# A short convolution's first tap on ScalarE in a two-layer block on one core

## Reference

```python
qkv = jax.nn.silu(causal_depthwise_conv(qkv, w_conv_qkv[i]))      # four taps along the tokens, one weight per channel
q, k, v = jnp.split(qkv, 3, axis=-1)                              # 16 heads of 128 each
q, k, v = l2norm(heads(q)), l2norm(heads(k)), heads(v)
beta = jax.nn.sigmoid(b_raw)
o_a = gated_delta_chunked(q, k, v, g_log, beta)                   # uses k and kb = k * beta
```

## Time and profile before

| | |
|---|---|
| median of 3 runs | 2548.47 us (2547.51 to 2551.29) |
| the profiled execution | 2548.92 us, its span 2547.4 us |
| PE busy | 2461.4 us, 97% of the span |
| DVE busy | 1629.1 us, 64% |
| ACT busy | 1155.0 us, 45% |
| POOL busy | 175.4 us, 7% |
| mean granted PE clock | 0.991 of full speed |

### The profile page before, as it was taken

The page is one execution under the profiler, slowest core; times in us unless marked ns, Lnnn a source line. Parts: engine busy times, 40 slices in busy tenths (PEclk is TensorE's granted clock), DMA queues, the critical chain, the costliest instruction groups (busy, mean ns, idle before and its releaser), DMA issues.

```text
span 2547.4 us, 34830 instructions
## 1 busy us (share of the span) xinstructions
PE 2461.4 (97%) x13453; PEld 2046.6 (80%) x13453; DVE 1629.1 (64%) x2146; ACT 1155.0 (45%) x1475; POOL 175.4 (7%) x254
## 2 busy tenths in 40 slices
PE   7999999988999999999999889999999999999997
PEld 6878878867888888788887778888888888888886
DVE  5899999678585766646546655656465544565554
ACT  5444444455353535334445454444444444443443
POOL 3000000153000101001000010000000000000000
PEclk9999999989999999999999999999999999999999
DMA  7566666445343344648655445655565655675563
GB/s 233 187 203 205 211 202 205 156 158 166 117 149 117 133 133 142 212 161 276 235 185 187 165 155 175 207 168 203 171 204 163 224 187 193 205 274 192 188 218 113
DMA packets 226899, 469.75 MB, mean 184 GB/s; under 512 B 12217, under 2 KB 13090, under 8 KB 225634
## 3 DMA queue, kind: packets, MB, share of 16 engines
q1 hardware_dynamic: 214018, 418.57, 49.5%
q0 software_dynamic: 12768, 49.59, 5.6%
HBM read 445.05 MB, written 23.07 MB: 184 GB/s over the span
## 4 chain that ended last, share of the span: by engine, by line
PE 70%; DVE 3%; ACT 2%; issue 1%; POOL 0%; DVEq 0%; ACTq 0%; POOLq 0%
PE acc L2119 60%; PE aux L2265 3%; PE aux L2149 1%; PE aux L2351 1%; PE aux L2355 1%; DVE w_lo L1376 1%; DVE cy L1632 0%; PE aux L2276 0%; ACT w_hi L809 0%; PE aux L2340 0%; PE aux L2350 0%; PE aux L2535 0%; PE aux L2534 0%; PE acc L2442 0%; ACT qT L1053 0%
## 5 line engine op out<-in xcount | busy, mean ns | idle before, releaser
L1376 DVE TENSOR_TENSOR w_lo<-raw,w_hi 128x1024 fp32r<-128x1024 f32 x790 | 973.0, 1235 | 817.1 <-ACT w_hi L809 805.6
L809 ACT CAST w_hi<-raw 128x1024 fp32r<-128x1024 f32 x790 | 827.0, 1051 | 1188.3 <-PE acc L2119 1176.0
L2119 PE MATMUL acc<-w_hi,r1h 128*128 128x512 f32 (+1 forms) x1920 | 764.1, 398 | 7.4 <-DVE r1l L1461 4.4
L2119 PE MATMUL acc<-w_lo,r1h 128*128 128x512 f32 (+1 forms) x1920 | 747.5, 389 | 0.0
L2119 PE MATMUL acc<-w_hi,r1l 128*128 128x512 f32 (+1 forms) x1920 | 747.4, 389 | 0.0
L2119 PE MATMUL acc<-w_hi,r2h 128*128 128x512 f32 x1216 | 477.5, 393 | 2.2 <-DVE w_lo L1376 1.9
L2119 PE MATMUL acc<-w_lo,r2h 128*128 128x512 f32 x1216 | 473.5, 389 | 0.0
L2119 PE MATMUL acc<-w_hi,r2l 128*128 128x512 f32 x1216 | 473.5, 389 | 0.0
L2119 PEld LDWEIGHTS acc<-w_hi,r1h 128*128 128x128 f32 x1920 | 362.6, 189 | 85.8 <-issue 5.1
L2119 PEld LDWEIGHTS acc<-w_hi,r1l 128*128 128x128 f32 x1920 | 362.1, 189 | 76.1
L2119 PEld LDWEIGHTS acc<-w_lo,r1h 128*128 128x128 f32 x1920 | 362.6, 189 | 69.9 <-issue 1.0
(11 more groups left out here) (442 smaller groups left out, 1591.3 us busy)
## 6 DMA issues: line engine op xcount, KB each, us to landing
raw<-in_w_in SPq DMA_DIRECT2D x264, 1024.0 KB, 5.0
raw<-in_w_out SPq DMA_DIRECT2D x32, 1024.0 KB, 4.9
raw<-in_w_br_b SPq DMA_DIRECT2D x16, 1024.0 KB, 4.9
raw<-in_w_br_a SPq DMA_DIRECT2D x16, 1024.0 KB, 5.3
raw<-in_w_ple_gate SPq DMA_DIRECT2D x16, 1024.0 KB, 4.9
raw<-in_w_o_mla SPq DMA_DIRECT2D x16, 1024.0 KB, 4.9
raw<-in_w_o_conv SPq DMA_DIRECT2D x16, 1024.0 KB, 4.9
raw<-in_w_q_b SPq DMA_DIRECT2D x8, 1024.0 KB, 5.1
```

The source lines that it names most:

```text
L809: nc.scalar.copy(w_hi[:, h % HL, 0:n], raw[:, k % RAW, x * HALF:x * HALF + n]).then_inc(hi_ready, 1)
L1376: V.tensor_tensor(w_lo[:, h % HL, 0:n], raw[:, k % RAW, x * HALF:x * HALF + n], w_hi[:, h % HL, 0:n].bitcast(F32), ALU.subtract).then_inc( ...
L2119: ins = T.matmul(acc[:, s, x, 0:n], a[:, kt0 + k, xs_], w[:, h % HL, at], start=start and k == 0 and m == 0, stop=stop and k == kts - 1 an ...
```

## The change

ACT writes the first tap of each convolution (tap 0) into `cy`, right behind the padding copies, in halves 10, 19 and 26. For n = 1 and 2 it first waits for `qk_square`, since DVE still has to sum the squares that lie in `cy`. DVE waits for `tap0_ready` in place of `cpad_ready` and does the 12 steps that are left, spread over the same halves. The small copies of the tap weights (`wq4`, three per group) go from DVE's half 0 to ACT's. DVE signals `ktok_ready` behind the scaled k and `kb_ready` behind k times beta; PE waits for the first ahead of the transposes of `ktok` and for the second ahead of those of `kb`. Four signals that occur once each become one counter, `small_done`; the order in which PE raises it is the order in which they were raised before.

```diff
@@ ScalarE
             def own(ph, hl, i, first):
+                if hl == 0:
+                    for n in range(3):
+                        c.inc(nc.scalar.copy(wq4[:, n], pc[:, bass.ds(i * GH, GH), R_SC + n:N_ROWS:3]))
...
+                for n, (evac, _, pad, (conv, conv_end), silu, back) in enumerate(OWN):
+                    if hl == conv - 1:
+                        if n:
+                            act.wait_ge(sem("qk_square"), i * 2 + n)
+                        c.wait()
+                        for h in range(GH):
+                            ins = A(cy[:, h], cpad[:, h, 0:TOK], ACT.Copy, scale=wq4[:, n, h, 0:1])
+                            if h < GH - 1:
+                                c.inc(ins)
+                        sig(ins, "tap0_ready", i * 3 + (n + 1))
@@ VectorE
             def own(ph, hl, i):
-                if hl == 0:
-                    for n in range(3):
-                        c.link(V.tensor_copy(wq4[:, n], pc[:, bass.ds(i * GH, GH), R_SC + n:N_ROWS:3]))
                 for n, (_, _, _, (conv, conv_end), silu, back) in enumerate(OWN):
                     if hl == conv:
-                        dve.wait_ge(sem("cpad_ready"), i * 3 + (n + 1))
+                        dve.wait_ge(sem("tap0_ready"), i * 3 + (n + 1))
                     if conv <= hl <= conv_end:
-                        steps, m = [(k, h) for k in range(SHORT) for h in range(GH)], conv_end - conv + 1
-                        for k, h in steps[16 * (hl - conv) // m:16 * (hl - conv + 1) // m]:
+                        steps, m = [(k, h) for k in range(1, SHORT) for h in range(GH)], conv_end - conv + 1
+                        for k, h in steps[len(steps) * (hl - conv) // m:len(steps) * (hl - conv + 1) // m]:
                             c.wait(GH - 1)
                             win, w = cpad[:, h, k:k + TOK], wq4[:, n, h, k:k + 1]
-                            if k == 0:
-                                c.inc(V.tensor_scalar(cy[:, h], win, w, None, ALU.mult))
-                            else:
-                                c.inc(V.scalar_tensor_tensor(cy[:, h], win, w, cy[:, h], ALU.mult, ALU.add))
+                            c.inc(V.scalar_tensor_tensor(cy[:, h], win, w, cy[:, h], ALU.mult, ALU.add))
...
                 if hl == 31:
                     dve.wait_ge(sem("cols_ready"), i + 1)
-                    c.link(V.tensor_tensor(th(ktok), th(ktok), over(col(2), DK), ALU.mult))
-                    c.link(V.tensor_tensor(th(kb), th(ktok), over(col(3), DK), ALU.mult))
-                    dve.sem_inc(sem("kb_ready"), 1)
+                    sig(V.tensor_tensor(th(ktok), th(ktok), over(col(2), DK), ALU.mult), "ktok_ready", i + 1)
+                    sig(V.tensor_tensor(th(kb), th(ktok), over(col(3), DK), ALU.mult), "kb_ready", i + 1)
@@ TensorE
             def delta(hl, dv, i=None):
                 if hl == 0:
+                    pe.wait_ge(sem("ktok_ready"), dv(1, 1))
+                    per_head_tr(0, ktok, "kT_tr")
                     pe.wait_ge(sem("kb_ready"), dv(1, 1))
-                    per_head_tr(0, ktok, "kT_tr")
                     pe.wait_ge(sem("vb_ready"), dv(1, 1))
                     per_head_tr(2, kb).then_inc(sem("kbT_tr"), 1)
```

More of the change, by code:

```diff
@@ L103 @@
 TR_GAINS, TR_NARROW, TR_ROWS = range(1, 4)
+SMALL_DECAYS, SMALL_MEAN, SMALL_RSTD, SMALL_P = range(1, 5)
 ROW_SLOT = P // KT
@@ L855, in decays_exp @@
             def decays_exp():
-                act.wait_ge(sem("gc_done"), 1)
+                act.wait_ge(sem("small_done"), SMALL_DECAYS)
                 n16 = TT * HEADS
@@ L977, in own @@
             def own(ph, hl, i, first):
-                for n, (evac, _, pad, (_, conv_end), silu, back) in enumerate(OWN):
+                if hl == 0:
+                    for n in range(3):
+                        c.inc(nc.scalar.copy(wq4[:, n], pc[:, bass.ds(i * GH, GH), R_SC + n:N_ROWS:3]))
+                for n, (evac, _, pad, (conv, conv_end), silu, back) in enumerate(OWN):
                     if hl == back + 1 and n < 2:
@@ L1083, in _ @@
                 if hl == 2:
-                    act.wait_ge(sem("mean_done"), 1)
+                    act.wait_ge(sem("small_done"), SMALL_MEAN)
                     sig(nc.scalar.copy(rows[:], X[:, 0, 0:TOK]), "rows_ready", 1)
                 if hl == 11:
-                    act.wait_ge(sem("rstd_rows"), 1)
+                    act.wait_ge(sem("small_done"), SMALL_RSTD)
                     act.wait_ge(sem("ln_centered"), NJ)
@@ L1151, in evac_square @@
                 act.wait_ge(acc_free[s], freed(ph, bl, i))
-            act.wait_ge(sem("p_tr"), 1)
+            act.wait_ge(sem("small_done"), SMALL_P)
             sig(nc.scalar.copy(pTh[:].rearrange("p a b -> p (a b)"), X[:, 2]), "p_hi", 1)
@@ L2190, in log_decays @@
                         ins = T.matmul(X[:, 3, at:at + HEADS], half_ones[:, n, :], glog[:, x], start=True, stop=True)
-                ins.then_inc(sem("gc_done"), 1)
+                ins.then_inc(sem("small_done"), 1)
             def u_transposed(ph, i):
@@ L2369, in _ @@
                         ins = T.matmul(X[:, 0, 0:TOK], ones_mean[:], y[:, kt], start=kt == 0, stop=kt == KT - 1)
-                    ins.then_inc(sem("mean_done"), 1)
+                    ins.then_inc(sem("small_done"), 1)
                 if 4 <= hl < 4 + NJ:
@@ L2383, in _ @@
                         ins = T.matmul(X[:, 1, x * P:(x + 1) * P], ones_mean[:], rdiag[:, x], start=True, stop=True)
-                    ins.then_inc(sem("rstd_rows"), 1)
+                    ins.then_inc(sem("small_done"), 1)
                 own(ph, hl, 0)
@@ L2423, in _ @@
                     ins = T.transpose(X[:, 2, a * TOK + x * P:a * TOK + (x + 1) * P], ptok[:, x, a * P:(a + 1) * P], ident[:])
-            ins.then_inc(sem("p_tr"), 1)
+            ins.then_inc(sem("small_done"), 1)
             ph = PH["MIX"]
```

## The result

| | before | after |
|---|---|---|
| median, lowest to highest, of 8 runs each, in turn on one chip | 2548.24 us (2547.32 to 2551.29) | 2555.28 us (2552.27 to 2556.96) |
| ratio, 95% interval | | 1.0029 (1.002 to 1.0038) |
| the profiled execution, its span | 2548.92, 2547.4 us | 2552.27, 2550.7 us |
| PE, DVE, ACT busy | 2461.4, 1629.1, 1155.0 us | 2463.7, 1614.3, 1176.3 us |
| mean granted PE clock | 0.991 | 0.990 |

The change makes the kernel slower by 7.0 us, 0.29%. DVE has 14.8 us less to do and ACT 21.3 us more, as intended; PE gains nothing from it.

A forecast was written before the change was run, and what follows sets the result against it. PE, busy for 97% of the span, was taken as the bound, so only its waits could change. +2.8 us (group 0) and +1.9 (groups 1 to 3) gave +4.7: 2553.6 for the execution, 2553.2 for the median, range 2548.5 to 2557.5.

The forecast's parts named there:

- +2.8 for group 0: Group 0: PE starts the decays 3.9 us late, less 0.3 of a wait and 0.8 from q and k.
- +1.9 behind it: Groups 1 to 3: the decays start later by about 0.6 us in each, +1.9 us in all.
- The rounding of half 30: Groups 1 to 3, on ACT: queued behind v's taps, which wait for DVE's sum of squares, it starts 2.27 us late.
- the prediction's own test: Groups 1 to 3: the forecast counts as wrong if the rounding of half 30 starts less than 2 us late.
- The price of the taps: On ACT: four taps of 128x256 with a per-partition scale take 1.65 us, from a range of 1.58 to 2.08.
- Group 0, q: PE's 10.8 us wait for q shrinks by 0.7 us; the next DVE step inherits the first taps' delay from POOL.
- POOL's hold is what matters: Rival, group 0: q's wait shrinks by some 3.5 us instead of 0.7, sum about +1.9, 2550.4 us; chance 0.16.
- Group 0, v: ACT's taps wait for the sum of squares; luh starts 3.9 us late, DVE's lul ends 4.05 late, PE's decays 3.9 late.
- PE's clock adds little: Group 0: a 4 us wait for v would cost about 1 us of clock, mostly while PE would wait for ktok anyway.
- ACT's wait is hidden: Rival, all groups: rounding three halves ahead takes up the 2.27 us, all removals count, −9, 2539.5 us; chance 0.09.
- Little of it shows: Rival: the late rounding is partly taken up, about +1, 2549.5 us; chance 0.10.
- The slower rival: Four taps take 2.08 us, 0.43 more in each of four chains, and group 0's w_lo loses time; +8.5, 2557 us; chance 0.15.

The follow-up runs named there:

- e1_again: The changed kernel measured once more with no edit, for its spread and a second profile: 2556.00 us, ratio 1.0033.
- e2_squares: The changed kernel with ACT's squares of q and k in tile kbe instead of cy, so the taps need not wait: 2547.18 us, ratio 0.9996.
- e3_wait: The kernel before, with only ACT's wait for qk_square added behind the padding copies; no tap moved: 2555.64 us, ratio 1.0029.
- e8_shift: The kernel before, with PE transposing the scaled k twice in each group: 2550.77 us, ratio 1.0015.
- e9_shift3: The kernel before, with PE transposing the scaled k three times in each group: 2553.88 us, ratio 1.0025.
- e5_split: The kernel before with only the split signal (ktok_ready, kb_ready); taps and weight copies stay on DVE: 2546.13 us, ratio 0.9997.
- e6_copies: The kernel of e5_split plus the three small weight copies per group on ACT; all taps on DVE: 2548.43 us, ratio 1.0.
- e7_best: The kernel of e2_squares with v's taps in group 0 alone back on DVE: 2544.59 us, ratio 0.9985.
- e4_v_on_dve: The changed kernel with all four taps of v back on DVE; the rest of the change stays: 2545.66 us, ratio 0.9991.

## Why the prediction came out as it did

**The mechanism was right, and its sum nearly so.** Forecast were +2.8 for group 0 and +1.9 behind it, 4.7 us; the stretches give 3.6 and 1.2, 4.8 us (5.0 in e1_again). That the sums agree to 0.1 us is luck: group 0 cost 0.8 more than forecast and the others 0.7 less. e2_squares and e3_wait show from both sides that ACT's wait for `qk_square` makes it. The chances were a little off: 0.53 went to a change within 0.2%, 0.38 to a slower one, and it is 0.29%.

**Groups 1 to 3, step by step.** Predicted and found: PE's wait for the gated output 1.31 and 1.37 us; for `ktok` 0.43 and 0.42; for the decays' operand 0.54 and 0.32. The wait for the convolved values fell from 0.77 to 0.45. The rounding of half 30 came 1.94 us late against the decays ahead (733.16 - 618.03 against 729.33 - 616.14), not 2.27: the sum of squares itself ended 0.55 us earlier, which fits DVE's fewer steps ahead of it but was not tested. By the prediction's own test (under 2 us is a sign of being wrong) this is just on the wrong side, without consequence: 0.4 us for each group instead of 0.6. PE's waits grew by only 0.5 of these 1.2 us (7.9 to 8.4 over the stretch), and the clock is 1.00 throughout in both kernels; the rest appears as PE's busy time, 407.95 us in place of 406.64 for the same 3463 matmuls. Sets of matmuls behind a wait are recorded a little longer, as the output's transposes (1.09 against 1.03) and the decays (1.10 against 1.02); that this makes the whole rest is not shown.

**The price of the taps** was 1.65 us and is 1.71 to 1.72. The Trainium skill (ScalarE: Activation LUTs, What ACT_TABLE_LOAD costs) gave an estimate of 1.69; the trace agrees to 0.03 us. The nearest row for such a price was in the earlier trace rows and not in the earlier trace rows: eight operations with a scale for each partition, from SBUF to SBUF, at half the columns, 2.45 us.

**Group 0, q.** Forecast -0.7; the wait is 10.2 us where it was 10.8. The rival "POOL's hold is what matters" fell. DVE in the changed kernel:

```profile
525.00 3.57 DVE L1640 SCALAR_TENSOR_TENSOR cy<-cpad,wq,cy 128x256 f32<-128x256 f32 x3
...
532.34 5.78 DVE L1640 SCALAR_TENSOR_TENSOR cy<-cpad,wq,cy 128x256 f32<-128x256 f32 x3
538.04 3.39 DVE L1765 SCALAR_TENSOR_TENSOR lnt<-lnt,lnsq 128x1024 f32<-128x1024 f32 x1
```

Three steps take 3.57 us where four first taps took 3.54, and three take 5.78 where four took 5.94: the delay passed to the next step, and behind the steps to L1765, which takes 3.39 us here and took 1.21 before. The Trainium skill (SBUF — State Buffer, two separate sides) says that a DVE operation with two SBUF inputs waits for the ports shared with POOL while a POOL operation that reads SBUF holds them. The trace agrees: beside POOL's L628 (2.56 us each) two single steps took 2.62 us each, where four take 1.67 us in group 1.

**Group 0, v.** Measured from the `szT` mark, `luh` starts 3.4 us late (130.19 against 126.82), POOL's last column 3.6 late (147.62 against 144.03), the decays 3.6. Forecast were 3.9 less the 0.8 of q and k for the same chain, so 3.1 at that mark. The 0.1 of k was not found, q gave 0.1 less, and the rest of the half microsecond lies between `luh` and POOL's columns. The wait of 0.3 for bf came back, but behind the mark.

**Where PE spent those 3.6 us was wrong in part.** PE's waits in group 0 grew only by 1.3 us (from 17.9 to 19.2, the same view for 478 to 622 us). The others were spent at the lower clock. Behind the starts of k's and v's transposes, before and after:

```profile
585.00:588.00 3.00, 3.00 (x19) 2.59 (x18) 1.42 (x2) 2.97 (x6) 0.00 (x0) 1.00 1.06 321
...
606.80:609.80 3.00, 2.94 (x17) 2.62 (x18) 2.02 (x3) 0.74 (x3) 2.69 (x4) 1.00 0.96 305
609.80:612.80 3.00, 2.08 (x15) 1.58 (x15) 2.01 (x3) 2.97 (x9) 1.12 (x2) 1.00 0.14 53
```

```profile
582.80:585.80 3.00, 3.00 (x10) 2.31 (x9) 1.49 (x2) 2.97 (x6) 0.00 (x0) 0.67 1.07 322
...
607.50:610.50 3.00, 2.99 (x14) 2.57 (x15) 1.21 (x1) 0.00 (x0) 2.83 (x3) 0.69 0.95 313
610.50:613.50 3.00, 3.00 (x15) 2.46 (x14) 2.45 (x2) 2.50 (x9) 2.10 (x4) 0.74 0.12 42
```

At 0.67, 0.69 and 0.74 of full speed in 3 us each, 1.0, 0.9 and 0.8 us are lost, where before the clock was full at these distances behind a wait; behind q's wait, shorter by 0.6 us, less was lost. The difference of the stretches leaves 2.3 us for it all. As predicted for v, this cost nothing on top: it filled time in which PE would have waited for a late chain, and at its end PE still waits 0.57 us for the decays' operand. That need not be so: in e3_wait, where the chain is less late, the lower clock behind v's wait costs 1.4 us.

**The step that failed is the last one**, from the trace's sum to the median: "PE's clock adds little". 2553.2 was forecast and 2555.28 measured. The mechanism adds 4.8 to 5.0 us to a kernel whose median is 2548.24, 2553.1. The remaining 2 us are of the kind that e1_again shows (2.6 us behind 1450 us, at unchanged waits). It is shown where they lie and that they are PE's lower clock in that execution. That the other executions of the changed kernel have them in the same place is argued from their times and mean clocks (0.988 or 0.989 in six of the eight, 0.990 in the profiled one, against 0.991 in nearly all of the kernel before), as only two were profiled. Why e3_wait and the changed kernel have them in nearly every execution, e8_shift in five of eleven, e9_shift3 in two and e5_split, which is neither later nor has the wait, in three, stays open; a later place in time alone does not bring them.

**The other rivals.** "ACT's wait is hidden" fell with the 3.06 us for which DVE waited. "Little of it shows" fell with e3_wait. The slower rival was right that more would be slow, but wrong on its cause, as the taps took 1.72 us and not 2.08.

**Where the expected gain went.** Work was moved from an engine that is 64% busy to one that is 45% busy. The Trainium skill (Perfetto Trace Analysis, Optimizing Scalar/DVE Operations) says that "if DVE is saturated, offloading some work to Scalar (or even GPSIMD) may make sense". DVE was not saturated here, and the work moved brought next to nothing: groups 1 to 3 gained 2.6 us with no tap moved (e6_copies) and 3.1 with all of them moved and unblocked (e2_squares), so the first taps on ACT, of which v's four took DVE 1.14 us, brought PE under 0.2 us a group.

## What to carry to other kernels

Before moving work to another engine, look at what it must wait for there and at what is queued behind it: a wait of 1.5 to 3 us for a shared scratch tile cost 5.2 us by itself (e3_wait, 1.4 of it by PE's clock), more than the 3.7 us that the best form of the change gains (e7_best), and another tile for the squares removed it. Split such a change into its parts before judging it; here the two smallest made the gain. When the effect is a few microseconds, compare stretches between marks of the two traces: medians of kernels whose edited stretches agree differed here by 2 to 3 us (e4_v_on_dve and e6_copies, 2545.66 and 2548.43).

## What the runs showed of the hardware

- Two executions of the changed kernel differ by where PE's lower clock falls: 30.3 or 32.0 us for the same instructions with the same waits, 1070.2 or 1071.1 for the rest of the program. Behind the same wait for `w_lo` (1.92 and 1.95 us) the first matmul took 0.47 us in the one and 0.75 in the other. The sets of times of e8_shift and of e5_split lie some 4 us apart.
- The length of PE's wait alone did not say what clock the matmuls behind it got. Eight transposes took 1.97 us behind a wait of 3.83 us (k's) and behind one of 3.58 us (v's, e3_wait), but 1.09 us behind one of 3.80 us (v's, changed kernel), where the 3 us from their start on had 0.69 of full speed all the same. Behind v's wait of 2.44 us, before, the clock stayed at 1.00.
- Three copies of 128x16 take ACT 0.44 us together, issued without a wait between them, and took DVE 0.81 (L1620), which waited for the end of each, so that moving them off a chain on DVE costs ACT next to nothing.
